# Projecting the expert queries of both token tiles at once, and alternating the key halves of the scores

## The reference

```python
q = (h @ w_pq).reshape(B, T, PEER_HEADS, 2, PEER_HALF)
s = jnp.einsum('bthcd,hckd->bthck', q, sub_keys)
top_s, top_i = lax.top_k(s, PEER_TOPK)   
cand = top_s[..., 0, :, None] + top_s[..., 1, None, :]
best_s, best_j = lax.top_k(cand.reshape(B, T, PEER_HEADS, PEER_TOPK * PEER_TOPK), PEER_TOPK)
expert = i1 * PEER_KEYS + i2
...
u = jnp.take(u_tab, ec, axis=0)
act = jax.nn.gelu(jnp.einsum('cd,ced->ce', hc, u), approximate=False)
v = jnp.take(v_tab, ec, axis=0)
return jnp.einsum('ce,ced->cd', (act * wc).astype(h.dtype), v)
```

## Time and profile before

| | us |
|---|---|
| median of 3 runs | 3473.19 (3470.31 to 3478.11) |
| the profiled execution | 3472.1 |
| its span, first to last instruction | 3470.0 |
| TensorE, VectorE, POOL, ScalarE busy | 2566.6, 2110.8, 1730.7, 531.0 |
| mean granted TensorE clock | 0.890 |
| HBM read | 1034.97 MB, 300 GB/s over the span |

### The profile page before, as it was taken

How to read it: one execution, slowest core, us unless ns; L and a number is a source line. 1 busy time by engine, 2 the same in 40 slices (tenths; PEclk the granted TensorE clock), 3 DMA queues, 4 the chain that set the end, 5 groups by cost and what they waited for, 6 DMA issues and landing times. The chain is left out here.

```text
span 3470.0 us, 27245 instructions
## 1 busy us (share of the span) xinstructions
PE 2566.6 (74%) x8111; PEld 1362.2 (39%) x8111; DVE 2110.8 (61%) x4260; ACT 531.0 (15%) x1146; POOL 1730.7 (50%) x1721
## 2 busy tenths in 40 slices
PE   8889986577858657785983577778888827777777
PEld 1465135355633535563653222223346602222223
DVE  0165846876664787666558986554427598664543
ACT  0131101000000110000221111212213201111111
POOL 0110164665545466643204677776721057777774
PEclk9979986689889668887986899999999859999999
DMA  8613597989869798986506899999971189999997
GB/s 293 218 51 113 205 400 246 353 320 352 316 246 399 247 338 319 355 314 243 187 1 260 317 409 409 408 409 409 409 276 55 40 329 392 409 409 409 409 409 315
DMA packets 361586, 1040.98 MB, mean 300 GB/s; under 512 B 35783, under 2 KB 90830, under 8 KB 360572
## 3 DMA queue, kind: packets, MB, share of 16 engines
q0 software_dynamic: 221952, 805.51, 60.1%
q1 hardware_dynamic: 137632, 231.64, 18.9%
q10 hardware_dynamic: 1884, 2.37, 0.2%
HBM read 1034.97 MB, written 4.44 MB: 300 GB/s over the span
## 5 line engine op out<-in xcount | busy, mean ns | idle before, releaser
L1786 PE MATMUL PS<-W,SCALE 128*128 128x512 f32 x1984 | 957.6, 613 | 420.2 <-DMA W<-in_peer_v,IDX 258.0
L1892 DVE CUSTOM_DVE_ANT_0 W<-W,PS 128x1024 f32<-128x1024 f32 x512 | 610.7, 1218 | 379.7 <-DMA W<-in_peer_u,IDX 378.6
L1786 PEld LDWEIGHTS PS<-W,SCALE 128*128 128x128 f32 x1984 | 347.3, 191 | 1026.8 <-ACT SCALE L1837 527.1
L1933 POOL DMA_INDIRECT W<-in_peer_u,IDX x512 | 487.8, 953 | 483.8 <-PE PS L299 274.3
L1933 POOL DMA_INDIRECT W<-in_peer_v,IDX x512 | 490.0, 957 | 172.2 <-issue 133.7
L1274 PE MATMUL PS<-XT,W 128*128 128x256 f32 x1408 | 326.8, 395 | 93.2 <-DMA W<-in_w_up 93.2
L340 DVE CUSTOM_DVE_ANT_0 ROWS<-ROWS,PROD 128x1024 f32<-128x1024 f32 x256 | 308.1, 1224 | 131.8 <-DMA ROWS<-in_peer_u,IDXS 130.6
L331 POOL DMA_INDIRECT ROWS<-in_peer_u,IDXS x256 | 325.9, 1273 | 115.0 <-issue 63.7
L361 DVE SCALAR_TENSOR_TENSOR PROD<-ROWS,COEF,PROD 128x1024 f32<-128x1024 f32 x256 | 329.0, 1285 | 52.8 <-DMA ROWS<-in_peer_v,IDXS 25.3
L1837 ACT ACTIVATE SCALE<-C,COEF 128x128 f32<-128x128 f32 x496 | 197.4, 401 | 970.0 <-PE PS L1786 951.0
L331 POOL DMA_INDIRECT ROWS<-in_peer_v,IDXS x256 | 297.7, 1163 | 96.0 <-issue 67.7
(11 more groups left out here) (284 smaller groups left out, 2202.0 us busy)
## 6 DMA issues: line engine op xcount, KB each, us to landing
W<-in_w_mod SPq DMA_DIRECT2D x24, 2048.0 KB, 8.2
W<-in_w_up SPq DMA_DIRECT2D x44, 1024.0 KB, 21.7
W<-in_w_in SPq DMA_DIRECT2D x21, 2048.0 KB, 18.3
W<-in_w_down SPq DMA_DIRECT2D x22, 1024.0 KB, 9.6
W<-in_w_o SPq DMA_DIRECT2D x6, 2048.0 KB, 9.8
W<-in_peer_wq SPq DMA_DIRECT2D x6, 2048.0 KB, 7.8
W<-in_w_out SPq DMA_DIRECT2D x4, 2048.0 KB, 11.0
W<-in_peer_u,IDX POOLq DMA_INDIRECT x512, 11.4
```

Of the source, the lines that this page charges most:

```text
L1786: ins = nc.tensor.matmul(PS[:, 4 + 2 * t + h, :], SCALE[:, i % NSCALE, :], row_slot(at[1, g])[:, h * 512:(h + 1) * 512], start=m == 0, sto ...
L1892: nc.vector.tensor_tensor_reduce(row_slot(n), row_slot(n), PS[:, 2 * t:2 * t + 2, :].rearrange("p n d -> p (n d)"), 1.0, 0.0, ALU.mult, AL ...
L1933: nc.gpsimd.indirect_dma_start(row_slot(n), None, tables[("peer_u_2", "peer_v_2")[v]], bass.IndirectOffsetOnAxis(IDX[:, t, m:m + 1], 0),). ...
```

## The change

The transposes of both tiles now come first. Then the projection takes both tiles at once: 256 tokens move, and a group holds two heads, so that there are four groups `("pq", g)` for a stage instead of four `("pq", t, j)`. The scores are made for one tile and four heads at a time (`half`), and the two key halves c alternate within it, each writing a bank of its own. The order is written out: groups 0, 1, 2, the scores of tile 0 and heads 0 to 3, group 3, and the three other score sets. ScalarE's copies follow in the same order, with a stepped output for the projection. The waits of SP and POOL name the new groups.

```diff
-                pe.wait_ge(xT_ready, 4 + t * 2 + 2)
-                for j in range(2):
-                    if t == 0:
-                        weights_in(pe, 6 + j)
-                    b = banks.take(picksT_ready, t * 2 + j + 1)
-                    for h in range(4):
-                        ins = matmul_rows(pe, b, (h * P, (h + 1) * P), lambda k: wslot(2 + j, DK, 512)[:, k, h * P:(h + 1) * P],
-                                          lambda k: XT[:, k, t * P:(t + 1) * P], DK)
...
-                for g in range(4):
-                    b = banks.take(score_read, t * 4 + g + 1)
-                    for i in range(4):
-                        h, c = (g // 2) * 4 + i, g % 2
-                        if i == 0:
-                            pe.wait_ge(picksT_ready, t * 2 + g // 2 + 1)
-                        ins = nc.tensor.matmul(PS[:, b, i * P:(i + 1) * P], B["QPT"][c * HD:(c + 1) * HD, t, h, :],
...
+            pe.wait_ge(xT_ready, 4 + 2 * TT)
+
+            def picks(g):
+                if g % 2 == 0:
+                    weights_in(pe, 6 + g // 2)
+                b = banks.take(picksT_ready, g + 1)
+                for h in range(2):
+                    o = (2 * g + h) % 4 * P
+                    ins = matmul_rows(pe, b, (h * S, (h + 1) * S), lambda k: wslot(2 + g // 2, DK, 512)[:, k, o:o + P],
+                                      lambda k: XT[:, k, :], DK)
...
+            def scores(t, half):
+                pe.wait_ge(picksT_ready, 2 * half + 2)
+                if t == 0 and half == 0:
                     pe.wait_ge(keysT_ready, 2)
...
+                bs = [banks.take(score_read, t * 4 + half * 2 + c + 1) for c in range(2)]
+                for i in range(4):
+                    for c in range(2):
+                        h = half * 4 + i
+                        ins = nc.tensor.matmul(PS[:, bs[c], i * P:(i + 1) * P], B["QPT"][c * HD:(c + 1) * HD, t, h, :],
                                                B["KPT"][c * HD:(c + 1) * HD, h, :], start=True, stop=True)
...
+            picks(0)
+            picks(1)
+            picks(2)
+            scores(0, 0)
+            picks(3)
+            scores(0, 1)
+            scores(1, 0)
+            scores(1, 1)
```

ScalarE (`stream_act`), SP and POOL:

```diff
+            def picks(g):
+                b = bank("pq", g)
+                nc.scalar.copy(B["QPT"][:, :, 2 * g:2 * g + 2, :].rearrange("p t h s -> p h t s"),
+                               PS[:, b, :].rearrange("p (h t s) -> p h t s", h=2, t=TT)).then_inc(picksT_ready, 1)
...
-                    used = {8: ("mix", 0, 1), 9: ("mix", 1, 1), 10: ("pq", 1, 0), 11: ("pq", 1, 1)}
+                    used = {8: ("mix", 0, 1), 9: ("mix", 1, 1), 10: ("pq", 1), 11: ("pq", 3)}
...
-                           lambda: groups.of("pq", TT - 1, 1))
+                           lambda: groups.of("pq", 3))
...
-                        pool.wait_ge(groups_done, groups.of("pq", TT - 1, 1))
+                        pool.wait_ge(groups_done, groups.of("pq", 3))
```

More of the change, by code:

```diff
@@ L668, in stream_pe @@
                     groups.at["hT", t, j, "bank"] = b
-                pe.wait_ge(xT_ready, 4 + t * 2 + 2)
-                for j in range(2):
-                    if t == 0:
-                        weights_in(pe, 6 + j)
-                    b = banks.take(picksT_ready, t * 2 + j + 1)
-                    for h in range(4):
-                        ins = matmul_rows(pe, b, (h * P, (h + 1) * P), lambda k: wslot(2 + j, DK, 512)[:, k, h * P:(h + 1) * P],
-                                          lambda k: XT[:, k, t * P:(t + 1) * P], DK)
-                    ins.then_inc(groups_done, groups.mark("pq", t, j))
-                    groups.at["pq", t, j, "bank"] = b
@@ L679, in stream_pe @@
-                if t == 0:
-                    pe.wait_ge(keysT_ready, 2)
-                for g in range(4):
-                    b = banks.take(score_read, t * 4 + g + 1)
-                    for i in range(4):
-                        h, c = (g // 2) * 4 + i, g % 2
-                        if i == 0:
-                            pe.wait_ge(picksT_ready, t * 2 + g // 2 + 1)
-                        ins = nc.tensor.matmul(PS[:, b, i * P:(i + 1) * P], B["QPT"][c * HD:(c + 1) * HD, t, h, :],
-                                               B["KPT"][c * HD:(c + 1) * HD, h, :], start=True, stop=True)
-                    ins.then_inc(groups_done, groups.mark("ps", t, g))
-                    groups.at["ps", t, g, "bank"] = b
+            pe.wait_ge(xT_ready, 4 + 2 * TT)
@@ new lines, in picks @@
+            def picks(g):
[6 more added lines that the diff above has]
+                                      lambda k: XT[:, k, :], DK)
+                ins.then_inc(groups_done, groups.mark("pq", g))
+                groups.at["pq", g, "bank"] = b
@@ new lines, in scores @@
+            def scores(t, half):
+                pe.wait_ge(picksT_ready, 2 * half + 2)
+                if t == 0 and half == 0:
+                    pe.wait_ge(keysT_ready, 2)
+                bs = [banks.take(score_read, t * 4 + half * 2 + c + 1) for c in range(2)]
[3 more added lines that the diff above has]
+                        ins = nc.tensor.matmul(PS[:, bs[c], i * P:(i + 1) * P], B["QPT"][c * HD:(c + 1) * HD, t, h, :],
+                                               B["KPT"][c * HD:(c + 1) * HD, h, :], start=True, stop=True)
+                        if i == 3:
+                            ins.then_inc(groups_done, groups.mark("ps", t, half * 2 + c))
+                            groups.at["ps", t, half * 2 + c, "bank"] = bs[c]
@@ L813, in stream_act, with scores @@
                     root(act, 1, 6, 1.0 / D, 1)
[L814 to L818, removed]
+            def picks(g):
+                b = bank("pq", g)
+                nc.scalar.copy(B["QPT"][:, :, 2 * g:2 * g + 2, :].rearrange("p t h s -> p h t s"),
+                               PS[:, b, :].rearrange("p (h t s) -> p h t s", h=2, t=TT)).then_inc(picksT_ready, 1)
+            def scores(t, half):
+                for g in range(2 * half, 2 * half + 2):
                     b = bank("ps", t, g)
-                    dst = B["SC"][t].rearrange("p (h c k) -> p h c k", c=2, k=EK)[:, (g // 2) * 4:(g // 2) * 4 + 4, g % 2, :]
+                    dst = B["SC"][t].rearrange("p (h c k) -> p h c k", c=2, k=EK)[:, half * 4:half * 4 + 4, g % 2, :]
                     nc.scalar.copy(dst, PS[:, b, :].rearrange("p (h k) -> p h k", h=4)).then_inc(score_read, 1)
+            picks(0)
+            picks(1)
+            picks(2)
+            scores(0, 0)
+            picks(3)
+            scores(0, 1)
+            scores(1, 0)
+            scores(1, 1)
         def softmax_act(act, B, t, h0, h1, done):
```

## The result

| | before | after |
|---|---|---|
| median of 4 runs each, us | 3474.02 (3470.31 to 3478.11) | 3519.14 (3514.57 to 3525.66) |
| the profiled execution, its span, us | 3472.1, 3470.0 | 3523.0, 3521.2 |
| mean granted TensorE clock | 0.890 | 0.883 |

The changed kernel is slower: ratio 1.0131, 95% interval 1.0108 to 1.0154, which is 45.1 us. The forecast was 43.4 us more, 3516 us.

A forecast was written before the change was run, and what follows sets the result against it. Latent stages were taken as bound by the chain first score, search, full-rate gathers; the context stage by two racing chains. 10.7 + 2 x 13.05 + 3 x 2.2 = 43.4 us more gave 3516 us, range 3504 to 3524.

The forecast's parts named there:

- part 1: Projection: 256-column records at 217.1 ns, 6.95 us per group, 27.79 instead of 29.12 us, saving 1.33 us per stage.
- Rival A: Projection: a record costs its weight load, 113.7 ns at any width; +10.4 us, 3484, or +3.8 at full clock; chance 3%.
- the milder case by the Trainium skill: Projection: width is cheap, both tiles in an estimated 17.5 us; whole 17.8 us slower with the clock, 3491; within 3%.
- part 2: Before the projection: waiting for H of tile 1, 6.86 us after tile 0's, starts it at 1822.86 instead of 1816.00.
- part 3: Latent stages: three groups, 20.84 us for 14.56, precede the first score; 2.2 us on to the search, 13.05 us later.
- part 4: After the first search: group 3 no longer holds POOL, row products come 13.05 us later, H copies and stepped output cost nothing.
- I take the latter: Latent stages' ends: POOL starts some 12.3 us later, row products 13.05; the products' 13.05 is counted.
- part 5: Context stage: search 20.6 us later, stage end 10.7 us later, without the clock cost.
- The slack of 9.9 us: Context stage: VectorE's 9.9 us of idling behind TensorE's chain is used up; without it the loss would be 20.6.
- part 6: Ahead of the first score: 5.8 us of TensorE idling lowers its clock, costing 2.2 us per stage, bounds 0.1 and 2.6.
- Rival B: All stages: TensorE's work sets the ends and the late search is made up for; 10.1 us faster, 3463; chance 3%.
- rival C: Latent stages: only the last projection's slot release counts, 1.9 us each, and searches catch up; +21 us, 3494; chance 3%.

The follow-up runs named there:

- experiment 4: Changed kernel with unread matmuls between the transposes of tile 0 and tile 1: with 12, 3687.30 us (ratio 1.0129); with 6, 3659.88 us (1.0076).
- experiment 5: Kernel before with key halves alternating: 3628.23 us (0.9993); changed kernel without alternation: 3519.78 us (1.0138); changed kernel repeated: 3517.08 us (1.0133).
- experiment 7: Kernel before, alternating, POOL sooner, latent tile 0 two heads at a time: 3456.30 us (0.9958); H of tile 0 also copied early: 3448.78 us (0.9938).
- experiment 6: Kernel before, halves alternating, tile 0's heads 0 to 3 projected and scored first: 3628.18 us (0.9995); POOL also begins sooner: 3614.95 us (0.9949).
- experiment 2: Kernel before with the change in the context stage alone, latent stages keeping the old code: 3655.33 us, ratio 1.0046.
- second kernel of experiment 6: Kernel before, halves alternating, tile 0's heads 0 to 3 first, POOL waiting for the projection only at gathers 9 and 13: 3614.95 us, ratio 0.9949.
- alternation alone: Kernel before with only the loop over the key halves turned inside out: 3628.23 us, ratio 0.9993.
- the kernel with quarters: Kernel before, halves alternating, latent tile 0 projected and scored two heads at a time, POOL waiting only at gathers 9 and 13: 3456.30 us, ratio 0.9958.

## Why the prediction was right

Time, range and sign were right (3519.14 in 3504 to 3524), and nearly all of the steps. That the sum came within 3 us is better than the interval of the measurement, 16 us wide, can vouch for; the marks are what bears the steps out. Point by point:

- **The width** (part 1). The forecast had 217.1 ns for a record of 256 columns and three groups in 20.84 us. At full clock they took 20.99 (experiment 4), 218.6 ns each. Rival A, a record that costs its weight load alone, is out, and with it the milder case by the Trainium skill (TensorE: Matmul & The Clock Gate, "Back-to-back issue gap"), whose 81 ns for 128 columns and 131 for 512 the trace doesn't bear out: it has 113.7 ns at 128 and 436 at 512 (experiment 4). The forecast's 17.5 us for that case is 14.56 us scaled by the ratio of those figures; taken as they stand, some 98 ns for each of 128 records, they give 12.5 us as an estimate, still further from the trace.
- **The wait for tile 1** (part 2). H of tile 1 came 6.88 us after tile 0's; TensorE idled 5.54 (forecast: some 5.8).
- **Three groups ahead of the score** (part 3). From the end of the third group to the search it took 1863.09 - 1860.86 = 2.23 us; forecast 2.2. Of the terms in it, 16 alternating records took 1.16 and not 0.9, hence about half of the gain between the bounds 1.41 and 0.91. The reason given was right in kind: in the changed kernel's trace these records start in pairs 6 to 7 ns apart, one pair every 112 ns, while with the halves in a row (experiment 5) most starts are 106 to 112 ns apart. That a pair is one record of each half is inferred; the trace doesn't name the half. The Trainium skill (TensorE: Matmul & The Clock Gate, "Part 3: Packing small matmuls — row/col tiling") gives about 4 ns between starts on different row groups; the trace is near that. The longer records were made up by copies that took 1.07 and not 1.13, with less idle time around them. What the step missed is that alternation hardly shortens the way to the search (by 0.07 us in experiment 5), because the two copies start no sooner.
- **Later groups** (part 4). The stepped copy costs nothing: 0.585 us at L829 with its stepped output, as the plain one did at L816. POOL's first gather is released by VectorE. One reason in this part holds only in part: "I take the latter because VectorE is the one without idle time there". Where the gathers run at 400 to 409 GB/s, as in the forecast's own trace, the ends did go with the products (experiment 7); on the chip with slower gathers, products 6.3 us earlier gained nothing (experiment 6). In this change gather and product are late by nearly the same, 15.7 and 16.0 us, so that the choice between them was worth 0.3 us and the result couldn't test it: that much was luck.
- **The context stage** (part 5). Forecast 10.7 with the clock apart, 12.9 with it; measured 13.3. The slack of 9.9 us was used up, and experiment 2 shows the stage alone with the same end.
- **The clock** (part 6). This is the mis-sized term. 2.2 us per stage was taken, 2.6 the upper bound, between projections after 4.15 and 7.16 us of idle time. Measured were 2.4 in the context stage and 3.0 in each latent one (experiment 4). The sum counted the projection alone; the eight transposes ahead of it ran at 1.2 GHz as well, 1.97 instead of 1.04 us.

With the clock term at 2.4 + 2 x 3.0 = 8.4 instead of 6.6, the sum is 45.2, and 45.1 was measured; so close a fit is chance, given that interval. Rival B, TensorE's work as the limit, is contradicted by the signs of all stages; rival C, in which the searches catch up in the latent stages, by ends that are 15.8 and 16.5 us later and not 1.9.

What stays open: how the 4.1 us between the latent stages come about in the profiled execution. TensorE is busy for 152.5 us there instead of 148.3, at a granted clock of 0.90 and 0.87 in its two halves instead of 0.93 and 0.90. The clock is a likely cause, but no run was made for it.

## What to carry to other kernels

Before two groups of work are merged for the sake of an engine, ask who waits for the first piece. Here a merge would save about 1 us of TensorE time per stage at full clock (29.12 for the 20.99 + 7.17 of experiment 4) and held back the search, the gathers and the products behind it by some 16; going the other way, to smaller first pieces, gained 24.5 us once the gathers and the copy of H were let go earlier too. And if a start should be moved, find every chain that ends in the same transfers, since moving one of them alone gained nothing in experiment 6.

## What was unexpected in the hardware

**The transposes pay for an idle TensorE too.** After 5.54 us without work, eight records of 128 columns took 1.97 us instead of 1.04, and the 96 of the projection 22.58 to 23.17 instead of 20.99. Six matmuls that nobody reads, in the gap, gave 2.4 to 3.0 us per stage back.

**TensorE stalled with no wait in sight.** In the second kernel of experiment 6 the first gather is issued while TensorE still projects tile 1. Its timeline there:

```profile
1838.41 13.66 PE L299 MATMUL PS<-XT,W 128*128 128x128 f32 x120 [1.11 <-ACT XT L819]
1853.03 0.47 PE L299 MATMUL PS<-XT,W 128*128 128x128 f32 x2 [0.95 <-issue]
...
1856.57 0.39 PE L299 MATMUL PS<-XT,W 128*128 128x128 f32 x2 [1.72 <-issue]
1858.71 0.57 PE L299 MATMUL PS<-XT,W 128*128 128x128 f32 x1 [1.75 <-issue]
1860.12 0.37 PE L299 MATMUL PS<-XT,W 128*128 128x128 f32 x1 [0.84 <-issue]
```

120 of the 128 records run at 114 ns each, and the last eight take until 1860.5, with gaps of 0.84 to 1.75 us in which the program has no wait. The 32 score records behind them take 4.48 us where alternation alone has 2.06. Both latent stages show it. A window of this kernel, and two of the kernel with quarters (columns as in the earlier trace rows):

```profile
1852.00:1856.00 4.00, 0.96 (x5) 0.78 (x5) 3.79 (x15) 0.00 (x0) 3.01 (x4) 1.00 0.90 350
```

```profile
1836.00:1840.00 4.00, 4.00 (x38) 4.00 (x38) 3.83 (x17) 0.59 (x1) 3.08 (x4) 1.00 0.90 299
1840.00:1844.00 4.00, 4.00 (x39) 4.00 (x38) 3.79 (x12) 0.00 (x0) 3.08 (x4) 1.00 1.00 380
```

At full granted clock TensorE was busy for 0.96 of 4 us in the first. The consequence was a late copy of H, for which the first product of this kernel stood 8.15 us:

```profile
1868.64 1.22 DVE L1903 CUSTOM_DVE_ANT_0 W<-W,PS 128x1024 f32<-128x1024 f32 x1 [8.15 <-ACT PS L1816]
```

Instructions that come through the DMA engines and queue behind the gathers would be an explanation, since the trace has DMA packets of a kind "instruction". But the quarters run the same projection beside equally full DMA engines without a gap, so full engines alone don't do it, at least on that chip; the stall was seen on the chip with slower gathers only, and the quarters ran on the other. It would need a delivery to fall into that stretch. Neither was tried, and the cause stays open.
